# Query projection by key lists of 128 columns with stationary weights, RMS applied to lists and scores, and 16 early rows

## The reference

```
x_lat = x_lat + m_lat[2] * (y_l @ w_out)              # output projection of the mixers
hf = modulate(rmsnorm_2(x_lat, norm_ffn), m_lat[3], m_lat[4])
x_lat = x_lat + m_lat[5] * peer_ffn(hf, wq, keys, u_tab, v_tab)
return rmsnorm_2(x_lat, norm_final)

# peer_ffn: 8 heads, each with two query halves of 128 columns, 128 keys for each half
q = (ht @ wq).reshape(n, 8, 2, 128)
s = einsum('nhpc,pkc->nhpk', q, keys)
s1, i1 = top_k(s[:, :, 0], 16); s2, i2 = top_k(s[:, :, 1], 16)
cand = s1[..., :, None] + s2[..., None, :]            # 256 candidates
sc, ci = top_k(cand, 16)                              # 16 experts for each head: 128 for each token
gate = softmax(sc)
a = einsum('nd,nhkd->nhk', x, u_tab[e]); w = gate * gelu(a)
out = einsum('nhk,nhkd->nd', w, v_tab[e])
```

## Time and profile before

| | |
|---|---|
| median of 3 runs | 3007.39 us |
| profiled execution | 3004.53 us, span 3002.8 us |
| TensorE / VectorE / ScalarE / GpSimd busy | 89% / 69% / 35% / 13% |
| granted TensorE clock, mean | 0.987 |
| output projection, last product starts | 1638.99 us |
| query projection, first product starts | 1647.17 us |
| first gather issued | 1695.49 us |

### The profile page before, as it was taken

The page is one execution under the profiler, slowest core; times in us unless marked ns, Lnnn a source line. Parts: engine busy times, 40 slices in busy tenths (PEclk is TensorE's granted clock), DMA queues, the critical chain, the costliest instruction groups (busy, mean ns, idle before and its releaser), DMA issues.

```text
span 3002.8 us, 28448 instructions
## 1 busy us (share of the span) xinstructions
PE 2666.8 (89%) x10050; PEld 1808.2 (60%) x10050; DVE 2061.1 (69%) x2509; ACT 1056.1 (35%) x1583; POOL 387.1 (13%) x401
## 2 busy tenths in 40 slices
PE   9999999999999999999999889877777777777773
PEld 7888888888888888788788654322222222222221
DVE  6675689899999987666556794676664554444446
ACT  5544453333333355635454422222222121111111
POOL 0000000000000000000000353211211221121112
PEclk9999999999999999999999999999999999999997
DMA  6554778889888874444354699999999999999997
GB/s 240 178 199 173 286 266 332 313 333 338 341 337 328 334 279 169 145 152 171 128 198 179 225 385 426 429 427 428 428 428 428 428 428 429 427 428 428 428 428 326
DMA packets 98942, 958.74 MB, mean 319 GB/s; under 512 B 11028, under 2 KB 11348, under 8 KB 13336
## 3 DMA queue, kind: packets, MB, share of 16 engines
q0 software_dynamic: 55552, 650.96, 52.2%
q1 hardware_dynamic: 43136, 305.91, 27.5%
q10 hardware_dynamic: 152, 0.53, 0.0%
HBM read 955.23 MB, written 2.13 MB: 319 GB/s over the span
## 4 chain that ended last, share of the span: by engine, by line
PE 59%; DMA 30%; DVE 7%; issue 2%; ACT 2%; POOL 0%; SPq 0%; POOLq 0%; DVEq 0%; ACTq 0%
DMA rows_g<-in_uv_tab_dram,idx 29%; PE bank L688 16%; PE bank L692 16%; PE bank L689 16%; PE bank L1230 6%; DVE rows_g L2692 4%; DMA raw<-in_wstream_dram 1%; PE bank L722 1%; PE bank L1045 0%; PE bank L990 0%; DVE split L1846 0%; PE bank L730 0%; ACT diag L1796 0%; ACT slot_w L1793 0%; POOL rows_g L662 0%
## 5 line engine op out<-in xcount | busy, mean ns | idle before, releaser
L1230 PE MATMUL bank<-rows_g,diag 128*128 128x512 f32 x2000 | 921.1, 606 | 267.9 <-ACT diag L1796 267.8
L2692 DVE CUSTOM_DVE_ANT_0 rows_g<-rows_g,XN 128x2048 f32<-128x2048 f32 x256 | 599.7, 2344 | 539.3 <-DMA rows_g<-in_uv_tab_dram,idx 537.4
L1230 PEld LDWEIGHTS bank<-rows_g,diag 128*128 128x128 f32 x2000 | 366.1, 192 | 822.7 <-issue 822.4
L1846 DVE TENSOR_TENSOR split<-raw,split 128x2048 fp32r<-128x2048 f32 x283 | 647.7, 2290 | 291.1 <-ACT split L1244 285.4
L1244 ACT ACTIVATE split<-raw 128x2048 fp32r<-128x2048 f32 x287 | 549.8, 1917 | 677.8 <-DMA raw<-in_wstream_dram 665.2
L688 PE MATMUL bank<-split,UH 128*128 128x512 f32 x1952 | 770.6, 395 | 4.9 <-DVE split L1846 4.4
L692 PE MATMUL bank<-split,UL 128*128 128x512 f32 x1952 | 760.8, 390 | 0.0
L689 PE MATMUL bank<-split,UH 128*128 128x512 f32 x1952 | 760.2, 389 | 0.0
L662 POOL DMA_INDIRECT rows_g<-in_uv_tab_dram,idx x274 | 302.2, 1103 | 1081.3 <-PE bank L1230 855.5
L688 PEld LDWEIGHTS bank<-split,UH 128*128 128x128 f32 x1952 | 367.0, 188 | 82.0 <-issue 2.6
L692 PEld LDWEIGHTS bank<-split,UL 128*128 128x128 f32 x1952 | 366.6, 188 | 77.0
(11 more groups left out here) (411 smaller groups left out, 1412.2 us busy)
## 6 DMA issues: line engine op xcount, KB each, us to landing
raw<-in_wstream_dram SPq DMA_DIRECT2D x288, 1024.0 KB, 4.8
ada_w<-in_ada_dram POOLq DMA_DIRECT2D x96, 1024.0 KB, 6.8
rows_g<-in_uv_tab_dram,idx POOLq DMA_INDIRECT x274, 26.2
X<-in_x_dram SPq DMA_DIRECT2D x4, 512.0 KB, 9.8
c_row<-in_c_rows_dram POOLq DMA_DIRECT2D x1, 2048.0 KB, 8.2
ctx_x<-in_ctx_dram POOLq DMA_DIRECT2D x1, 2048.0 KB, 10.4
gb<-mod_rows POOLq DMA_DIRECT2D x2, 1024.0 KB, 5.8
pool_t<-in_pool_t_dram POOLq DMA_DIRECT2D x1, 1024.0 KB, 5.1
```

The costliest lines, as they stand in the source:

```text
L1230: mm = pe.matmul(bank[4 * b + c], diag[:, n % DIAGS, :], v[:, c * CW:(c + 1) * CW], start=n in (0, SUMS_0), stop=n + 1 in (SUMS_0, len(SUMS)))
L1846: dve.tensor_tensor(WL[:, n % SLOTS_W, :], raw[:, n % SLOTS_W, :], WH[:, n % SLOTS_W, :].bitcast(F32), ALU.subtract).then_inc(lo_ready, 1)
L2692: dve.tensor_tensor_reduce(row(g), row(g), x, 1.0, 0.0, ALU.mult, ALU.add, dots[:, b, s:s + 1]).then_inc(sem("dot_done"), 1)
```

## The change

- The stream of the query weights is laid out by lists: list c holds all 2048 rows of 128 query columns (one half of a head), again 1 MB. The weights are now the stationary operand and the activations the moving one, with 258 columns: 256 tokens and two columns that hold the shift. The result comes out with query columns on partitions, so q_tok and its transposes are gone.
- X is multiplied by the row sc_row and turned un-normed. The parts of the first three tiles are turned within the last tile of the output projection (`last_output_tile`). The last tile's chunk runs block 0 before block 1, so VectorE can begin with block 0.
- The RMS enters later: q x rms = (scaled X) . w + rms x (shift . w), which `query` makes in one operation from PSUM, and the scores are multiplied by 1 / rms as ScalarE copies them.
- XN2 is modulated in one operation for each block (two passes in place of four).
- POOL_LO and stay_warm are gone; VectorE makes all low parts.
- 16 early rows (all of the first head) in four homes; the first choice is at m = 2, the second at m = 10, and the dots are spread anew (EARLY_DOTS).

```
-EARLY, LATE = 12, 6
-EARLY_HOMES = ((2, 0), (2, 1), (PAIRS, 0))
-EARLY_DOTS = (0, 0, 0, 0, 0, 0, 1, 2, 1, 2, 1, 2, 1, 2, 0, 0)
+EARLY, LATE = 16, 6
+EARLY_HOMES = ((2, 0), (PAIRS, 0), (PAIRS, 1), (2, 1))
+EARLY_DOTS = (0, 0, 0, 0, 0, 1, 1, 2, 1, 1, 0, 1, 2, 1, 3, 3)
...
+            def list_part(c, k0, k1):
+                s = (S_WQ + c) % SLOTS_W
+                o = q_bank(c)[:, 0:T + SHIFT]
+                for k in range(k0, k1):
+                    w = slice(k * P, (k + 1) * P)
+                    pe.matmul(o, WH[:, s, w], UHS[:, k, :], start=k == 0, stop=False)
+                    pe.matmul(o, WL[:, s, w], UHS[:, k, :], start=False, stop=False)
+                    mm = pe.matmul(o, WH[:, s, w], ULS[:, k, :], start=False, stop=k == KT - 1)
+                if k1 == KT:
+                    mm.then_inc(split_used, 1)
+            def list_scores(c):
+                pe.wait_ge(sem("q_t_ready"), c + 1)
+                if c >= 2:
+                    pe.wait_ge(sem("key_s_ready"), NB * (c - 1))
+                for b in range(NB):
+                    mm = pe.matmul(score_bank(c)[:, b * NKEY:(b + 1) * NKEY], q_t[c % 2][:, span(b)], keys[:, c % 2, :],
+                                   start=True, stop=True)
+                mm.then_inc(sem("key_ps"), 1)
...
+            def first_list():
...
+                for r in range(2):
+                    pe.wait_ge(sem("u_ready"), KT * 4 + CK * (r + 1))
+                    list_part(0, CK * r, CK * (r + 1))
+                scaled_turned(3)
+                pe.wait_ge(sem("u_ready"), KT * 4 + CK * 3)
+                list_part(0, CK * 2, CK * 3)
+                rms_spread()
+                pe.wait_ge(sem("u_ready"), KT * 5)
+                list_part(0, CK * 3, KT)
+            def lists():
+                first_list()
+                for c in range(1, LISTS):
+                    pe.wait_ge(lo_ready, S_WQ + c + 1)
...
+                    else:
+                        pe.wait_ge(sem("q_t_ready"), c - 3)
+                    at = SCORES_AT[c - 1] if c <= len(SCORES_AT) else KT
+                    list_part(c, 0, at)
+                    list_scores(c - 1)
+                    if at < KT:
+                        list_part(c, at, KT)
+                list_scores(LISTS - 1)
...
+            def modulated(b):
+                dve.scalar_tensor_tensor(XN2[:, b, :], XN2[:, b, :], rinv[:, b:b + 1], sh_row[:, :], ALU.mult, ALU.add).then_inc(
+                    sem("xn2_ready"), 1)
+            def query(c):
+                dve.wait_ge(split_used, S_WQ + c + 1)
...
+                ps = q_bank(c)
+                dve.scalar_tensor_tensor(q_t[c % 2][:, :], rms_row[:, :], ps[:, T:T + 1], ps[:, 0:T], ALU.mult, ALU.add).then_inc(
+                    sem("q_t_ready"), 1)
...
+            for m in range(LISTS):
+                if m != 2:
                     lo(S_WQ + m + LEAD)
+                if m == 1:
+                    modulated(0)
+                    lo(S_WQ + m + LEAD + 1)
+                if m == 2 or m == 10:
+                    for _ in choose(0, 0, 0 if m == 2 else 1, 1):
                         pass
+                if m == 3:
+                    modulated(1)
                 for g in range(sum(EARLY_DOTS[:m]), sum(EARLY_DOTS[:m + 1])):
+                    if g == 0:
+                        dve.wait_ge(sem("xn2_ready"), NB)
                     dot(g, XN2[:, 0, :])
+                query(m)
```

More of the change, by code:

```diff
@@ L421, in build @@
         hot = view("hot", "C", 2048 + GH * TOPK * TOPK, [GH, TOPK, TOPK])
+        q_t = [view(f"q_t{i}", "C", 2048 + TOPK * TOPK + 2 * TOPK * TOPK * i, [T]) for i in range(2)]
+        rms_row = view("rms_row", "C", C2["mask"], [T])
         top_v = view("top_v", "MISC", 0, [2 * GH, TOPK])
@@ L674, in products @@
             def products(n, banks, k0, nk, i, per, ah, al, blocks=NB, first=True, last=True, each=None):
[L676 to L679, removed]
+                if i is not None or n:
+                    pe.wait_ge(lo_ready, lin(n + 1, i, per))
                 wh, wl = WH[:, n % SLOTS_W, :], WL[:, n % SLOTS_W, :]
@@ L1166, in last_turned @@
                 yield
[L1168 to L1180, removed]
+            linear_among(S_OUT2, Q_OUT2, 0, OUT_TILES - 1, last_turned(), ready=lambda m: (sem("y2_ready"), CK * (m + 1)))
@@ L1181, in queries_turned, with scaled_turned @@
+            def scaled_turned(r):
+                pe.wait_ge(sem("xs_ready"), r + 1)
                 if r >= 2:
                     pe.wait_ge(sem("u_ready"), KT * 4 + CK * (r - 1))
[L1183 to L1204, removed]
-                            mm = pe.matmul(DB[2 + b][:, hp * NKEY:(hp + 1) * NKEY], q_t[:, hp, span(b)],
-                                           keys[:, hp % 2, :], start=True, stop=True)
-                        mm.then_inc(sem("key_ps"), 1)
@@ L1209, in _, with last_output_tile @@
-            stay_warm(40)
-            queries_turned(0)
-            queries_turned(1)
-            linear_among(S_WQ, Q_WQ, 0, OUT_TILES, queries(), ready=u_parts(4, 1),
-                         each=lambda k: (sem("u_ready"), KT * 4 + k + 1))
+                turn_part(r, XN2, DB[2 * (r % 2):2 * (r % 2) + 2])
+            def last_output_tile():
+                n, q = S_OUT2 + CPT * (OUT_TILES - 1), Q_OUT2 + OUT_TILES - 1
+                pe.wait_ge(acc_free_act, q + 1)
+                pe.wait_ge(acc_free_dve, q + 1)
+                for m in range(CPT - 1):
+                    products(n + m, LAST_ACC, m * CK, CK, None, 0, UH, UL, first=m == 0, last=False)
+                    scaled_turned(m)
+                m = CPT - 1
+                pe.wait_ge(lo_ready, n + m + 1)
+                wh, wl = WH[:, (n + m) % SLOTS_W, :], WL[:, (n + m) % SLOTS_W, :]
+                for b in range(NB):
+                    t = slice(b * P, (b + 1) * P)
+                    for k in range(CK):
+                        w = slice(k * CW, (k + 1) * CW)
+                        pe.matmul(LAST_ACC[b], UH[:, m * CK + k, t], wh[:, w], start=False, stop=False)
+                        pe.matmul(LAST_ACC[b], UH[:, m * CK + k, t], wl[:, w], start=False, stop=False)
+                        mm = pe.matmul(LAST_ACC[b], UL[:, m * CK + k, t], wh[:, w], start=False, stop=k == CK - 1)
+                    mm.then_inc(sem("last_out_ps") if b == 0 else split_used, 1)
@@ L1215, in _ @@
+            last_output_tile()
+            lists()
             for n, g in enumerate(SUMS):
@@ L2857, in layout @@
     put(S_OUT2, chunks(np.concatenate([mixed[D_SGU + D_ML:], mixed[:D_SGU + D_ML]])))
-    put(S_WQ, chunks(first["peer_wq_2"]))
+    put(S_WQ, first["peer_wq_2"].reshape(KT, P, LISTS, P).transpose(2, 1, 0, 3))
     def down_cols(x):
```

253 lines of the change are left out of this document (129 added, 124 removed).

## The result

The changed kernel takes 3023.15 us, the median of 4 runs (3022.3 to 3026.7), against 3006.32 for the kernel before in the same session; the ratio is 1.0064, 95% interval [1.0052, 1.0075]. It is 0.6% slower, where 2993 us was predicted. The profiled execution took 3022.57 us, its span is 3020.8 us, and the granted clock is 0.989 (0.987 before).

What follows compares the result with a forecast made beforehand. Gathers bound the late stretch: the end is T, plus 2.47 us for each unit not yet moved, plus 14.3. T gives -4.7 and four more units -9.9, together -14.6: 3007.4 - 14.6 = 2993 us, range 2982 to 3006.

Steps and rivals of the forecast that it cites:

- Layout (258 columns a step, 8-byte shifts) ... at nothing: Rows of 258 columns cost nothing, hidden by TensorE's 6 us a list; about 1 us a list if that failed.
- E: Time at which the query projection's list stage begins on TensorE, predicted at 1642.3 us.
- The turns within the last output tile: Three transposes moved into the last output-projection tile, where TensorE is the bound, put E 3.1 us later.
- Narrow products: List products on TensorE start 0.114 us apart, 128-wide weight loads hidden beneath them; 5.48 us for a list's 48.
- the third rival: Narrow products' weight loads don't hide: 3015 us at half a load bare, 3055 wholly bare; 8%.
- the bound taken for 0.13: Upper bound of the forecast: narrow products 0.13 us apart put the 12th dot 5 us later; with late landing, 3001 us.
- VectorE's walk: VectorE and TensorE followed through the lists: first choice done at E + 27.7, 12th dot at E + 102.7.
- T: Time from which gathers run at full rate: from 1755 to 1750.3 us (E + 108), worth -4.7 us.
- four more units moved: Early rows move 16 units (rows of 2048 floats on 128 partitions) before T, not 12: 4 x -2.47 = -9.9 us.
- Slower: Outcome slower by over 0.2%, through narrow products' weight loads that don't hide (3015 or 3055 us); 8%.

Runs made afterwards that it cites:

- e6: The whole change with UH and UL at the old distances for wide products, rows of 258 only in the lists, low row 0 kept elsewhere: 2994.12 us, 0.9965.
- e5: Kernel before with the moved arena and rows of 256, UH and UL shifted so their distances to the weight slots are 32768 and 16384 again: 3005.27 us, 0.9997.
- e14: As e5, with UH alone 256 bytes earlier (distance 33024) and UL at its old distance: 3003.58 us, 0.9997.
- e2: Kernel before with only the changed kernel's moved arena, rows of 256 (UH at 33024, UL at 16512 bytes): 3028.19 us, 1.0081.
- e8: As e6, with the lists' moving operand 256 columns wide and the two shift columns left out, so it fetches other rows: 2997.1 us, 0.9969.
- e7: As e6, with 12 early rows in three homes instead of 16 in four: 2993.36 us, 0.9958.
- e3: The changed kernel with UH and UL in rows of 256 until the lists, rows of 258 only for the lists: 3027.99 us, 1.0080.
- e10: As e5, with UH and UL both 64 bytes earlier (distances 32832 and 16448): 3015.35 us, 1.0034.
- e4: As e2, with UH and UL 8 bytes later: 3032.48 us, 1.0095.
- e11: As e5, with UH and UL both 32 bytes earlier (distances 32800 and 16416): 3040.51 us, 1.0114.
- e13: As e5, with UH alone 32 bytes earlier (distance 32800): 3038.14 us, 1.0118.
- e1: Kernel before with the changed arena and UH and UL in rows of 258 words, shift columns unused: 3034.48 us, 1.0101.

## Why the prediction was wrong

**The step that failed** is "Layout (258 columns a step, 8-byte shifts) ... at nothing". It was covered with TensorE's 6 us a list, that is, looked at only within the lists. The layout holds for all 5472 wide products ahead of them, where TensorE is the bound, and there it costs 26 to 29 us. The larger figure is 1668.20 in the changed kernel against 1639.43 in e6, which differs from it only in where UH, UL and one low row lie, in the rows' length ahead of the lists and in when the shift columns are written; 2.6 of it are how much sooner e6's execution stands at the gate rows' load than that of the kernel before (1529.50 against 1532.08 us), though both have free distances. e5 and e14 against e2 show the cost without any of the change.

In the sum of the profiled spans: predicted -14.6, measured +18.0, a miss of 32.6. E gives 25.9 of it: 23.8 are there at the gate rows' load, 2.4 the layout adds from there to E, and 0.3 come off for the next point; the rest, 6.7, lies between E and the last landing, 1338.3 us apart where the prediction had 1331.6.

**The turns within the last output tile.** Expected to put E 3.1 later than before (1642.3). In e6 it is 1639.4, but that execution was 2.6 ahead of the one before already at the gate rows' load, the same work in both:

```profile
1529.50 1.15 POOL L658 DMA_DIRECT2D gb<-mod_rows  x2 [151.19 <-DVE P L2475]
```

From this load to E it is 107.1 us in the kernel before and in e5, and 109.9 in e6 (112.3 in the changed kernel). So the turns cost 2.8 us, and this term was right within 0.3.

**Narrow products.** Predicted 0.114, measured 0.120 (23 steps from 1668.20 to 1670.96). The load does lie beneath the running product, and the third rival, the bare load, falls. By the Trainium skill's rule that a load overlaps running matmuls only when the row group differs ("TensorE: Matmul & The Clock Gate"; it stands in section "The mechanism", not in the one that the prediction names), the loads would have been bare; these runs disagree. The same section also lets a load go ahead that targets the background weight buffer, which the prediction left out. The remaining 0.006 don't come from the shift columns (e8), and what they are stays open. They make 16 x 48 x 0.006 = 4.6 us for the stage, within the bound taken for 0.13.

**VectorE's walk** held within 2 us: the first index comes at E + 28.6 (predicted 27.7), the 12th dot ends at E + 104.7 (102.7), and no dot is stretched (mean 2.292 us). Behind that it was off: the 16th dot ends at E + 116.5 (112.9), and the last list at E + 108.7 (102.3, with late chunks 105.3). The chunks' median landing was 6.4 us, as taken (6.5), but 10.3 at the worst; low parts waited 17.8 us for ScalarE, and TensorE waited 14.0 us for queries, at most 7.7, where 5.1 and 2.2 were expected.

**T and the number moved.** The prediction put T at E + 108 with 16 units moved, 5 us behind the last early row's issue, although its own least landing time was 7.6 us. In fact the first pair is issued only at 1776.9 us, E + 108.7, as four gathers of 2 to 3 us each stand ahead of it on GpSimd. The rate is near the full one (9 tenths of it up to 1780 us) from about 1771.5 us, E + 103.3, with 12.5 units, all by early rows, and at E + 108 = 1776.2 it is 14.4 units (at 1775 us 522.34 MB are left, 498.1 units, and 1.2 us go by): 1.6 units short, 4.0 us. The last 2.7 are a rate of 2.4725 us a unit in place of 2.467. So "four more units moved" is only in small part true: the homes wait for dots that stand behind the second choice, the DMA engines rest from 1755 to 1760, and rows 13 to 16 are issued 3 to 11 us ahead of the first pair. They move at a time when pairs would move as well. e7 shows it: without them nothing is lost.

**The sum with the layout cured.** e6 has a span of 2991.7 where the prediction's own sum for the profiled span is 2988.2, and its median of 2994.1 stands beside the predicted 2993. That is partly luck, as E is 2.9 earlier in that execution, mostly by the 2.6 above, and the stage behind it 6.4 longer than predicted (2977.39 - 1639.43 = 1338.0). The gain over before has a source of which the prediction was right: the stage from E to the last landing shortens from 1349.3 to 1338.

**The rivals.** None had this mechanism. "Slower" had 8%, for another reason; that the measured time lies between its two prices (3015 and 3055) is chance.

## What to carry to other kernels

When an edit moves or widens a buffer that TensorE reads, price it over every product that reads it in the whole kernel, not over the stage for which it was made, and keep the distance between the stationary operand's buffer and the moving one's, or measure the new one; a padding of a few words ahead of the buffer is all it took here. The cheapest check is the mean duration of the same product group before and after, in a stage that the change doesn't touch. And a row that is fetched early counts only if it can land before the full rate begins: look at when its home comes free, not at how many there are.

## What the runs showed of the hardware

The spacing of products with a fully hidden weight load depends on where the two operands lie to each other: 0.2267 us at distances of 32768 and 16384 bytes, and 0.2323 in the changed kernel. Moving UL by 128 bytes against the slots costs 24.6 us (with UH 256 off), UH by 32 bytes 34 us, UH by 256 nothing, and UH and UL by 64 each 11 us. Moving all of them together by 64 bytes costs nothing (e5); other shifts of the whole weren't tried. A start off a multiple of 64 bytes (from the arena's start) isn't needed for the cost, as e2, e3 and e10 have none, but e4, e11 and e13 have one, and a part of theirs may be due to it. e2 against e14 and e13 against e5 also change the distance between UH and UL; in e10 and e11 that is the old one, and time is lost all the same. In rows of 256 columns a given pair of buffers has the same distance modulo 512 bytes in all products; in rows of 258 it shifts by 8 bytes with each k-step, so that a free start could hold for few of them (e1: +30.5 us). The Trainium skill, "TensorE: Matmul & The Clock Gate", section "Step-by-step: what each phase is for", says that TensorE has two independent read ports, so that loading the next weights doesn't take read bandwidth from the running product. Here the place of what is loaded makes the running product longer (line 690, which doesn't use UL: 390 to 396 ns), while the recorded load beneath it keeps its 188 ns. Whether the load meets TensorE's own read of the slot, or a read or write of the slots by another engine, and what the cost is at other distances than those above, wasn't tried.
